# Expert biases put into PSUM by ScalarE ahead of the products, expert items of 96 rows, and the overflow branch moved behind the output store

## The chip, the cores and the metric

The kernel runs on one core of one Trainium2 chip. The metric is the time on the device, in microseconds (us), of one execution; each version is judged by the median of several runs. PE is TensorE's matmul unit, PEld its weight load, ACT is ScalarE, DVE is VectorE, POOL is GpSimd, SP is SyncE, which issues most DMAs.

## The reference, cut to what matters

One hybrid encoder layer on 512 tokens of width 1024, in float32: two kinds of attention, an output projection, and then a mixture of 32 experts of which each token uses 4. Only the last stage matters here:

```python
def expert_rows(args):
    xe, e = args
    hh = xe @ w1[e] + b1[e]
    glu = jnp.minimum(hh[:, :D_FF], SWIGLU_LIMIT)
    lin = jnp.clip(hh[:, D_FF:], -SWIGLU_LIMIT, SWIGLU_LIMIT)
    act = glu * jax.nn.sigmoid(SWIGLU_ALPHA * glu) * (lin + 1.0)
    return act @ w2[e] + b2[e]
```

`w1[e]` is 1024 x 2048 and `w2[e]` 1024 x 1024, both float32, so an expert has 12.58 MB of weights. Each expert's rows are summed into their tokens with the router's weights, and a last RMSNorm gives the output. There are 512 x 4 = 2048 (token, expert) pairs, 64 an expert on average; the router's choices, counted with the reference on its own inputs, give the fullest expert 88.

## The kernel before, in words

**Items.** The mixture is done in items, one expert with up to P = 128 of its tokens each: 32 main items (`MAIN`) and, only if some expert has more tokens than that, 15 overflow items (`REST`, `OVER`) behind a branch on `novi`. An item has 24 pieces of 128 x 1024 weights: 16 of `w1` and 8 of `w2`. For float32 accuracy each piece is split: ACT casts it to `stage_hi` (L783), DVE subtracts that from the raw piece to give `stage_lo` (L1203), and PE makes six matmuls of 512 columns (`multiply`, L2182 to L2191): hi x hi, lo x hi, hi x lo, two banks each. There are 4 stage buffers; ACT may cast piece j when PE has used piece j - 4. SP loads 1 MB chunks (two pieces) into a ring of 12 slots, each when DVE has split what was in its slot (`load_body`, L494 to L507); so a chunk is asked for about one item before its use.

**Order of an item t on each engine** (j counts pieces in `body`, pieces 0 to 15 are of `w1`, 16 to 23 of `w2`):
- PE: first bias matmuls (`bias_1`, L2150 to L2159: one 0/1 selector per bank, 32 rows deep, `start=True`), pieces 0 to 8, eight transposes of the previous item's activations (`turn_a`, L2147), pieces 9 to 15, eight transposes of the next item's gathered rows (`turn_x`, L2139), pieces 16 to 23, which belong to the previous item's second product.
- ACT: the casts, and behind piece 3 the weighted result of item t - 2 (`y_evac`, L1093), behind 12 `a_evac` (L1079), behind 19 `gate(t)` (L1085), behind 21 `x_evac` (L1063, L1066).
- DVE: the subtractions, and behind piece 1 `gated` (L1644), behind 5 `weights` (L1612), behind 7 the bias selector `select1` (L1607), behind 12 and 21 `turned_lo` (L1596), behind 18 the two clips that empty the first product's banks (L1632, L1636).
- POOL: gathers the next rows by an indirect DMA from `tn_scratch` (L655) and adds results into `x_scratch` by an indirect DMA (L666).

The biases b1 of all experts lie in SBUF as `bias1`, loaded by eight DMAs (L486) and split by ACT (L998) and DVE (L1506) before the mixture.

**Before the first item** the normalised rows `tn` are stored to `tn_scratch` tile by tile (L516), and the first gather waits for all of these stores. SP issues the loads of chunks 4 and 5 just ahead of the last of them (L511 to L516).

**The end.** The last item's result is kept in two parts and added by one-hot matmuls (`last_expert`, L2290) instead of by a scatter. Every engine reads `novi` and branches over the overflow items; then SP waits for POOL's `all_scattered` (L580), loads the four 128-row tiles of `x_scratch` (L582), DVE adds PE's sums (L1756), ACT takes the squares and roots (L1185, L1187), DVE scales (L1763) and SP stores (L585). In the last main item `gated` stands behind piece 23 (L1704) and `y_evac` behind piece 3 of the tail loop (L1159), after both halves of `a_evac`.

Of the kernel before, what the change touches and what calls it, by code (L numbers as in the profile page):

```python
# [20 lines left out]
F32 = mybir.dt.float32  # L21
# [30 lines left out]
OVER = S * TOPK // P - 1  # L52
# [78 lines left out]
def build(nc, x, norm1_g, w_in, b_f, g_fox, g_sb, w_out, norm2_g, w_router, b_router, w1, b1, w2, b2,  # L131
# [6 lines left out]
    with ExitStack() as ctx:  # L138
# [32 lines left out]
        gtab = sb("gtab", [P, ITEMS], I32)  # L171
        wtab = sb("wtab", [P, ITEMS])
        seltab = sb("seltab", [P, ITEMS + OVER])
        eidtab = sb("eidtab", [1, 16], I32)
        novi = sb("novi", [1, 1], I32)
        gidx = sb("gidx", [P, 1], I32)
        sidx = sb("sidx", [P, 1], I32)
        wcol = sb("wcol", [P, 1])
        last_rows = sb("last_rows", [P, 1])
# [47 lines left out]
        bias1 = over("bias1", [P, D], F32R, room_at)  # L227
        wdT = over("wdT", [P, S], F32R, room_at + 4096)
        sel1 = over("sel1", [P, P], F32R, room_at + 6144)
        sel1b = over("sel1b", [P, P], F32R, room_at + 6656)  # L230
        onehot = over("onehot", [P, S], F32R, room_at + 7168)
# [7 lines left out]
        ohslot = over("ohslot", [P, 16, P], F32R, qk_at + 16 * S)  # L239
        over_slot = in_slot("over_slot", [P, 16, P], F32R, 8)  # L240
# [8 lines left out]
        b1raw = slot(9)[:, 0:D]  # L249
# [5 lines left out]
        y_hi = act_hi[:, 2 * D:3 * D]  # L255
        y_lo = act_lo[:, 2 * D:3 * D]
        g2b = slot(8)[:, 0:D]
        small = slot(8)[:, D:2 * D]
        gath = qk2[:, 0, :]
        glu = qk2[:, 1, :]  # L260
        lin = qk2[:, 2, :]
        sig = qk2[:, 3, :]
        yout = qk2[:, 4, :]
# [22 lines left out]
        counts = part(2007, 32)  # L286
        most = part(2039, 1)
# [20 lines left out]
        minus, prow = cols[:, 16:17], cols[:, 17:18]  # L308
# [15 lines left out]
        g2_in, bias_in, gf_in = sem("g2_in"), sem("bias_in"), sem("gf_in")  # L324
# [26 lines left out]
        bias_hi, bias_lo = sem("bias_hi"), sem("bias_lo")  # L351
# [6 lines left out]
        sel1_r, sel1_used, clipped, sig_done, act_made = (sem(n) for n in ("sel1_ready", "bias1_added", "clipped", "sig_done", "act_made"))  # L358
# [90 lines left out]
        def _(sp):  # L449
# [78 lines left out]
            for c in range(SLOTS):  # L528
# [3 lines left out]
                if c == 1:  # L532
                    sp.wait_ge(bias_lo, 2)
# [16 lines left out]
            sp.dma_start(gfb, norm_f_g.rearrange("(a d) -> a d", a=1).partition_broadcast(P)).then_inc(gf_in, 16)  # L550
            sp.wait_ge(over_known, 1)
            n_over = sp.value_load(novi[0:1, 0:1], min_val=0, max_val=1)
            with sp.If(n_over > 0):
                sp.wait_ge(over_ready, 1)
# [4 lines left out]
                for c in range(KT):  # L559
                    z = moe_slot(c)  # L560
                    sp.wait_ge(*MAIN.freed(E - 1, c + 4))
                    sp.dma_start(slot(z), w1_d[bass.ds(e0, 1), c].rearrange("e p n -> p (e n)")).then_inc(full[z], 16)
                ew1, ew2 = expert(1), expert(0)
                for c in range(SLOTS):
                    load_body(ew1, ew2, c, REST.freed(0, c) if c < 4 else REST.freed_first(c - 4))
# [1759 lines left out]
```

## Time and profile before

| | us |
|---|---|
| median of 3 runs | 1477.76 |
| lowest, highest | 1477.41, 1479.73 |
| the profiled execution, its own time | 1478.53 |
| span of its instructions | 1476.8 |
| mean granted clock of TensorE | 0.993 of full |

The profiled execution is 0.8 us above the median; 1.7 us of its time lie outside the span. A time at the head of a timeline row is counted from the start of the span, and a row with xN merges N instructions in a row: its second number runs from the start of the first to the end of the last. A matmul's duration includes its pipeline, so the distance between starts tells its cost, not the duration.

### The profile page before, as it was taken

The page shows a single profiled execution, that of the slowest core. Times are in us where ns is not written, and L with a number is a line of the kernel's source. Part 1 is how long each engine was busy: PE and PEld are TensorE (multiplying, and loading weights), DVE is VectorE, ACT ScalarE, POOL GpSimd, SP SyncE. Part 2 cuts the span into 40 slices and gives each one's busy share as a digit, 9 for nine tenths or more (in the row PEclk, how much of TensorE's full clock was granted, in tenths as well). Part 3 has the DMA queues.
Part 4 walks back from the last instruction along what each step waited for, and adds up shares of the span by engine and source line. Part 5 has one row for each costly group of instructions (what it writes and reads, how often), then busy time and mean ns, then how long its engine had stood idle before and what let it go on. Part 6 is the DMA issues. An engine that isn't in the chain of part 4 may idle for free.

```text
span 1476.8 us, 22343 instructions
## 1 busy us (share of the span) xinstructions
PE 1448.6 (98%) x7069; PEld 1180.6 (80%) x7069; DVE 1323.5 (90%) x1520; ACT 1114.6 (75%) x1345; POOL 325.4 (22%) x179
## 2 busy tenths in 40 slices
PE   9999999999999999999999999999999999999996
PEld 7777787787888888888888888888888888888884
DVE  5778656569999999999999999999999999999997
ACT  5668545357888888888888888888888888878885
POOL 3000000141322222222222233233222222222210
PEclk9999999989999999999999999999999999999998
DMA  8021122369999999999999999999999999999963
GB/s 258 22 65 57 30 94 67 129 225 418 417 383 384 378 378 374 375 370 376 375 369 375 374 369 380 365 371 389 367 361 373 373 378 369 369 372 379 370 220 125
DMA packets 100074, 451.32 MB, mean 306 GB/s; under 512 B 13443, under 2 KB 25731, under 8 KB 67266
## 3 DMA queue, kind: packets, MB, share of 16 engines
q1 hardware_dynamic: 90706, 434.16, 76.8%
q0 software_dynamic: 9328, 16.64, 4.5%
q8 instruction: 23, 0.38, 0.1%
q14 instruction: 17, 0.14, 0.0%
HBM read 444.66 MB, written 22.54 MB: 316 GB/s over the span
## 4 chain that ended last, share of the span: by engine, by line
PE 85%; DVE 7%; ACT 3%; DMA 2%; issue 2%; POOL 0%; SPq 0%; POOLq 0%; ACTq 0%; DVEq 0%
PE zpair L2189 46%; PE bank L2189 23%; PE bank L1889 2%; PE bank L1777 2%; PE bank L2139 2%; PE bank L2147 2%; PE bank L1779 2%; PE bank L1778 2%; DVE stage_lo L1203 1%; DVE lbuf L1283 1%; PE zpair L2158 1%; DVE pt_lo L1292 1%; DMA tn_scratch<-qk 1%; ACT stage_hi L783 1%; DMA ring<-x_scratch 0%
## 5 line engine op out<-in xcount | busy, mean ns | idle before, releaser
L1203 DVE TENSOR_TENSOR stage_lo<-ring,stage_hi 128x1024 fp32r<-128x1024 f32 x796 | 945.9, 1222 | 37.9 <-ACT stage_hi L783 8.3
L783 ACT CAST stage_hi<-ring 128x1024 fp32r<-128x1024 f32 x796 | 828.2, 1054 | 169.8 <-PE zpair L2189 139.0
L2189 PE MATMUL zpair<-stage_hi,act_hi 128*128 128x512 f32 x1024 | 322.5, 396 | 0.0
L2189 PE MATMUL zpair<-stage_lo,act_hi 128*128 128x512 f32 x1024 | 316.2, 390 | 0.4 <-DVE stage_lo L1203 0.3
L2189 PE MATMUL zpair<-stage_hi,act_lo 128*128 128x512 f32 x1024 | 316.0, 390 | 0.0
L2189 PEld LDWEIGHTS zpair<-stage_lo,act_hi 128*128 128x128 f32 x1024 | 192.1, 188 | 41.8 <-DVE stage_lo L1203 1.3
L2189 PEld LDWEIGHTS zpair<-stage_hi,act_lo 128*128 128x128 f32 x1024 | 192.2, 188 | 40.9
L2189 PEld LDWEIGHTS zpair<-stage_hi,act_hi 128*128 128x128 f32 x1024 | 187.2, 188 | 43.4 <-issue 7.9
L662 POOL COPY sidx<-gtab 128x1 int32 (+1 forms) x31 | 122.4, 3947 | 378.2 <-ACT qk L1093 378.2
L2189 PE MATMUL bank<-stage_hi,act_hi 128*128 128x512 f32 x512 | 161.2, 396 | 0.0
L2189 PE MATMUL bank<-stage_hi,act_lo 128*128 128x512 f32 x512 | 158.6, 391 | 0.0
L2189 PE MATMUL bank<-stage_lo,act_hi 128*128 128x512 f32 x512 | 157.8, 389 | 0.0
L666 POOL DMA_INDIRECT x_scratch<-qk,sidx x31 | 129.6, 4179 | 25.0 <-POOL sidx L662 25.0
L2189 PEld LDWEIGHTS bank<-stage_lo,act_hi 128*128 128x128 f32 x512 | 96.1, 188 | 21.1 <-DVE stage_lo L1203 0.4
L2189 PEld LDWEIGHTS bank<-stage_hi,act_lo 128*128 128x128 f32 x512 | 96.4, 188 | 20.5
L2189 PEld LDWEIGHTS bank<-stage_hi,act_hi 128*128 128x128 f32 x512 | 94.0, 189 | 17.6
L651 POOL COPY gidx<-gtab 128x1 int32 (+1 forms) x31 | 6.1, 198 | 402.8 <-PE bank L2139 402.8
L1596 DVE TENSOR_TENSOR act_lo<-bank,act_hi 128x512 fp32r<-128x512 f32 x128 | 82.3, 683 | 4.9 <-ACT act_hi L1063 3.5
L1777 PE MATMUL bank<-act_hi,stage_hi 128*128 128x512 f32 x184 | 76.3, 415 | 1.9 <-DVE v_lo L1247 1.9
L1779 PE MATMUL bank<-act_hi,stage_lo 128*128 128x512 f32 x184 | 72.0, 391 | 0.0
L1778 PE MATMUL bank<-act_lo,stage_hi 128*128 128x512 f32 x184 | 71.9, 391 | 0.0
L675 POOL TENSOR_TENSOR qk<-ring 128x1024 f32<-128x1024 f32 x3 | 8.1, 2725 | 273.0 <-DVE ring L1352 273.0
(297 smaller groups left out, 1450.9 us busy)
## 6 DMA issues: line engine op xcount, KB each, us to landing
ring<-in_w SPq DMA_DIRECT2D x384, 1024.0 KB, 8.0
ring<-in_w_in SPq DMA_DIRECT2D x12, 1024.0 KB, 5.3
ring<-in_w_out SPq DMA_DIRECT2D x4, 1024.0 KB, 4.9
xs_all<-in_x SPq DMA_DIRECT2D x4, 512.0 KB, 6.5
ring<-in_x SPq DMA_DIRECT2D x4, 512.0 KB, 3.7
tn_scratch<-qk SPq DMA_DIRECT2D x4, 512.0 KB, 3.5
x_scratch<-ring SPq DMA_DIRECT2D x4, 512.0 KB, 3.8
ring<-x_scratch SPq DMA_DIRECT2D x4, 512.0 KB, 6.7
```

The costliest lines, as they stand in the source:

```text
L662: nc.gpsimd.tensor_copy(sidx[:], gtab[:, i:i + 1] if isinstance(i, int) else gtab[:, bass.ds(i, 1)]).then_inc(sidx_copied, 1)
L666: nc.gpsimd.indirect_dma_start(out=x2_d[:, :], out_offset=bass.IndirectOffsetOnAxis(ap=sidx[:, 0:1], axis=0), in_=yout, in_offset=None, bo ...
L783: nc.scalar.copy(dst, src).then_inc(split_hi, 1)
L1203: nc.vector.tensor_tensor(dst, src, hi_ap.bitcast(F32), ALU.subtract).then_inc(split_lo, 1)
L1596: nc.vector.tensor_tensor(dst_lo[:, 4 * h:4 * h + n, :], bank[6 + h][:, 0:n * P].rearrange("p (k t) -> p k t", k=n), dst_hi[:, 4 * h:4 * h ...
L1777: pe.matmul(dst, w_hi, m_hi, start=start, stop=False)
L1778: pe.matmul(dst, w_hi, m_lo, start=False, stop=False)
L1779: return pe.matmul(dst, w_lo, m_hi, start=False, stop=stop)
L1889: mm = pe.matmul(obank[m][:, kb * P:S], w[:, ph % 2, kb, :], x[:, m, 4 * kb:3 * kb + TT, :].rearrange("p i q -> p (i q)"), start=kb == 0 a ...
L2139: mm = pe.transpose(bank[6 + k // 4][:, k % 4 * P:(k % 4 + 1) * P], gath[:, k * P:(k + 1) * P], identF[:])
L2147: mm = pe.transpose(bank[6 + k // 4][:, k % 4 * P:(k % 4 + 1) * P], lin[:, k * P:(k + 1) * P], identF[:])
L2189: mm = pe.matmul(bank[b0 + h][:], w[:, k, :], m[:, j % STAGES, h * BANK:(h + 1) * BANK], start=start and w is T_hi and m is stage_hi, stop ...
```

## The change

- A row of b1 is no longer selected by matmuls. SP loads it for each item with two DMAs that spread 4 KB each over 96 partitions (`load_b1`), and ACT copies it into the four banks of the first product (`seed`), behind pieces 20 and 22 of the item before. PE's products then add onto it: none of them has `start=True`. At the beginning a few matmuls with `start=True` over those banks (`arm`) replace as many of `keep_busy`.
- Items have 96 rows (CAP) in place of 128. Tables, gathers, transposes, clips and copies cover 96 rows; copies of transposed rows are 384 columns wide in place of 512. The 512-column matmuls of `multiply` keep all 128 columns of their stationary tiles.
- `bias1`, `sel1`, `seltab` and what makes them are gone. `body` on PE is one loop, not two.
- The end of the kernel is done at once after the main items; reading `novi` and the branch follow the store of the output. SP waits for the last main scatter itself. `gated` of the last item moves ahead of its piece 23's end (behind piece 22), `y_evac` ahead of the second half of `a_evac`.

```diff
+CAP = 96
-OVER = S * TOPK // P - 1
+OVER = S * TOPK // CAP
@@ SP
-            sp.wait_ge(split_lo, W_IN_PIECES + 8)
-            for g in range(4):
-                for r in (32 * g, 32 * g + 16):
-                    sp.dma_start(b1raw[r:r + 16, :].rearrange("p (h n) -> p h n", h=2),
-                                 b1[0][:, g * BANK:(g + 1) * BANK].rearrange("(h e) n -> e h n", h=2)).then_inc(bias_in, 16)
+            def load_b1(e, i):
+                wait(sp, b1_set, 2 * i)
+                row = b1[0][e:e + 1, :] if isinstance(e, int) else b1[0][bass.ds(e, 1), :]
+                for h in range(2):
+                    sp.dma_start(b1b[h][0:CAP, :], row[:, h * D:(h + 1) * D].partition_broadcast(CAP)).then_inc(b1_in, 16)
...
                     sp.wait_ge(oproj, 16)
                     for c in (4, 5):
                         load_w1(0, c, moe_slot(c))
+                    load_b1(0, 0)
                 sp.wait_ge(tn_ready, t + 1)
...
                 if c == 2:
+                    load_b1(1, 1)
...
             with sp.Fori(2, E) as t:
                 for c in range(SLOTS):
                     load_body(t, t - 1, c, MAIN.freed(t - 1, c))
+                    if c == 1:
+                        load_b1(t, t)
...
+            sp.wait_ge(split_lo, MAIN.split(E - 1, W1P + W2P - 1))
+            sp.wait_ge(scattered, 16 * (E - 1))
+            totals(0)
             sp.wait_ge(over_known, 1)
             n_over = sp.value_load(novi[0:1, 0:1], min_val=0, max_val=1)
@@ ACT
-            act.wait_ge(bias_in, 128)
-            nc.scalar.copy(bias1[:], b1raw).then_inc(bias_hi, 1)
...
+            def seed(i, h):
+                act.wait_ge(b1_in, i * 32 + 32)
+                nc.scalar.copy(zpair[h][0:CAP], b1b[h][0:CAP, :].rearrange("p (b n) -> p b n", b=2)).then_inc(b1_set, 1)
...
                         if j == 19:
                             gate(t)
+                        if j == 20 and not last:
+                            seed(t + 1, 0)
                         if j == 21 and not last:
                             x_evac(t + 1)
+                        if j == 22 and not last:
+                            act.wait_ge(clipped, t * 2 + 2)
+                            seed(t + 1, 1)
...
                     if j == 2:
-                        act.wait_ge(used, ub + 24 * n - 8)
+                        y_evac(q0 + n - 2, ub + 24 * n - 8)
                         a_evac(q0 + n - 1, (1,))
-                    if j == 3:
-                        y_evac(q0 + n - 2, ub + 24 * n - 8)
@@ DVE
-            nc.vector.scalar_tensor_tensor(out=bias1[:], in0=bias1[:].bitcast(F32), scalar=minus, in1=b1raw,
-                                           op0=ALU.mult, op1=ALU.add).then_inc(bias_lo, 2)
-            nc.vector.tensor_copy(sel1[:], seltab[:, 0:1].to_broadcast([P, P])).then_inc(sel1_r, 1)
...
-                        if j == 7 and not last:
-                            select1(t + 1, both)
...
+                        if j == 22 and last:
+                            gated(t)
-                gated(q0 + n - 1)
@@ PE
+            def arm(b):
+                for h in range(2):
+                    mm = pe.matmul(bank[b][:, 2 * P * h:2 * P * (h + 1)], identB[:], masks[:], start=h == 0, stop=h == 1)
...
-                    mm = pe.transpose(bank[6 + k // 4][:, k % 4 * P:(k % 4 + 1) * P], gath[:, k * P:(k + 1) * P], identF[:])
+                    mm = pe.transpose(bank[6 + k // 4][:, k % 4 * CAP:(k % 4 + 1) * CAP], gath[:, k * P:(k + 1) * P], identF[0:CAP, 0:CAP])
...
-                    else:
-                        bias_1(t, halves)
                     pe.wait_ge(xT_lo_r, t * 2 + (1 if first else 2))
                     for j in range(W1P):
+                        if j < 2:
+                            pe.wait_ge(b1_set, t * 2 + j + 1)
```

## Rows read from the trace of the kernel before

**Rows 1.** The page, busy time of each engine

```profile
PE 1448.6 (98%) x7069; PEld 1180.6 (80%) x7069; DVE 1323.5 (90%) x1520; ACT 1114.6 (75%) x1345; POOL 325.4 (22%) x179
```

**Rows 2.** The page, the chain that ended last, by engine

```profile
PE 85%; DVE 7%; ACT 3%; DMA 2%; issue 2%; POOL 0%; SPq 0%; POOLq 0%; ACTq 0%; DVEq 0%
```

**Rows 3.** Timeline of PE over one item: start, us, engine, line, operation

```profile
881.08 0.61 PE L2189 MATMUL bank<-stage_lo,act_hi 128*128 128x512 f32 x2
881.63 0.50 PE L2158 MATMUL zpair<-bias,sel 32*128 32x512 f32 x4
...
883.57 0.63 PE L2189 MATMUL zpair<-stage_hi,act_hi 128*128 128x512 f32 x2
...
904.90 1.04 PE L2139 MATMUL bank<-identF,qk 128*128 128x128 f32 x8
...
907.16 0.62 PE L2189 MATMUL bank<-stage_hi,act_hi 128*128 128x512 f32 x2
...
916.24 0.61 PE L2189 MATMUL bank<-stage_lo,act_hi 128*128 128x512 f32 x2
916.79 0.51 PE L2158 MATMUL zpair<-bias,sel 32*128 32x512 f32 x4
```

**Rows 4.** Timeline of PE before the first item

```profile
311.67 1.04 PE L2077 MATMUL zpair<-pay,ohslot 128*128 128x32 f32 x8
```

**Rows 5.** Timeline of ACT in the same item, in brackets its idle time

```profile
907.28 1.06 ACT L1085 ACTIVATE qk<-qk 128x1024 f32<-128x1024 f32 x1 [1.12 <-DVE qk L1632]
908.24 1.98 ACT L783 CAST stage_hi<-ring 128x1024 fp32r<-128x1024 f32 x2
910.13 0.57 ACT L1063 CAST act_hi<-bank 128x512 fp32r<-128x512 f32 x1
...
911.09 4.15 ACT L783 CAST stage_hi<-ring 128x1024 fp32r<-128x1024 f32 x4
...
917.85 1.26 ACT L1093 ACTIVATE qk<-bank,wcol 128x512 f32<-128x512 f32 x2
```

**Rows 6.** Timeline of DVE in the same item

```profile
905.96 1.28 DVE L1632 TENSOR_SCALAR qk<-zpair 128x512 f32<-128x512 f32 x2
...
911.76 1.28 DVE L1596 TENSOR_TENSOR act_lo<-bank,act_hi 128x512 fp32r<-128x512 f32 x2
912.96 4.62 DVE L1203 TENSOR_TENSOR stage_lo<-ring,stage_hi 128x1024 fp32r<-128x1024 f32 x4
917.50 1.22 DVE L1644 SCALAR_TENSOR_TENSOR qk<-qk 128x1024 f32<-128x1024 f32 x1
918.63 4.62 DVE L1203 TENSOR_TENSOR stage_lo<-ring,stage_hi 128x1024 fp32r<-128x1024 f32 x4
```

**Rows 7.** Windows: busy of PE, PEld, DVE, ACT, POOL; clock; DMA share; GB/s

```profile
881.00:916.70 35.70, 35.70 (x168) 29.04 (x166) 34.70 (x37) 29.27 (x32) 9.50 (x4) 1.00 0.99 374
1425.00:1426.00 1.00, 1.00 (x6) 0.84 (x5) 1.00 (x2) 0.64 (x2) 0.00 (x0) 1.00 0.80 266
```

**Rows 8.** DMA from 330 to 345 us: rate, and us to landing

```profile
DMA packets 960, 6.23 MB, mean 416 GB/s; under 512 B 169, under 2 KB 169, under 8 KB 231
...
ring<-in_w SPq DMA_DIRECT2D x7, 1024.0 KB, 21.7
```

**Rows 9.** DMA of the whole run: KB each, us to landing

```profile
ring<-in_norm_g SPq DMA_DIRECT2D x1, 512.0 KB, 4.3
```

**Rows 10.** The chain in order of time, before the first item

```profile
310.75 8.61 DMA tn_scratch<-qk
```

**Rows 11.** Timeline of the end

```profile
1442.49 1.09 PE L2147 MATMUL bank<-identF,qk 128*128 128x128 f32 x8 [0.79 <-DVE qk L1644]
...
1446.48 1.28 ACT L1093 ACTIVATE qk<-bank,wcol 128x512 f32<-128x512 f32 x2
...
1456.90 0.10 POOL L772 MEMSET gidx<- 128x1 int32 x1 [5.39 <-issue]
...
1457.09 2.29 SPq L582 DMA_DIRECT2D ring<-x_scratch  x4
```

More of the change, by code:

```diff
@@ L285, in build @@
         w_lo = part(916, 16)
-        counts = part(2007, 32)
-        most = part(2039, 1)
+        counts = part(2013, 32)
+        most = part(2045, 1)
         pick = part(952, 256).rearrange("p (a e) -> p a e", e=E)
@@ L750, in last_scatter @@
                 pool.wait_ge(y_ready, E)
+                for t in range(TT):
+                    pool.wait_ge(fin_in[t], 16)
                 nc.gpsimd.tensor_copy(sidx[:], gtab[:, E - 1:E]).then_inc(sidx_copied, 1)
@@ L1103, in turns @@
                     return 16 * (loads_before(z) + k)
+                if b == MOE0:
+                    seed_first()
+                else:
+                    seed(q0, 0)
+                    seed(q0, 1)
                 for j in range(W1P):
@@ L1648, in run_items @@
                 ub = b - OPROJ_PIECES
-                both = run is REST
-                if run is REST:
-                    select1(q0, both)
                 for j in range(W1P):
@@ L2194, in run_items @@
                 q0, n, b, T0 = run.first, run.n, run.base, run.turn0
-                low, high = ((0,), (1,)) if run is MAIN else ((0, 1), (0, 1))
                 if b == MOE0:
-                    pe.wait_ge(bias_lo, 2)
-                    pe.wait_ge(sel1_r, 1)
-                    bias_quarters((4, 5, 2, 3), range(4))
+                    for z in (4, 5, 2):
+                        arm(z)
+                    arm(3).then_inc(armed, 1)
                     pe.wait_ge(tables, 1)
@@ L2202, in run_items @@
                     weight_table((0, 1))
-                    keep_busy(0, 3)
+                    keep_busy(0, 1)
+                    arm(0)
                     pe.wait_ge(counts_read, 1)
-                else:
-                    bias_1(q0, low)
                 turn_x(q0)
@@ L2209, in run_items @@
                     weight_table((2,))
-                    keep_busy(0, 6)
+                    for _ in range(3):
+                        arm(0)
                 pe.wait_ge(xT_lo_r, 2 * q0 + 1)
                 for j in range(W1P):
+                    if j < 2:
+                        pe.wait_ge(b1_set, 2 * q0 + j + 1)
                     if j == W2P:
@@ L2217, in run_items, with body @@
                         turn_x(q0 + 1)
+                        pe.wait_ge(wt_added, 1)
+                        arm(1).then_inc(armed, 1)
                 if b != MOE0:
                     turn_x(q0 + 1)
-                def body(r, halves, first=False, last=False):
+                def body(r, first=False, last=False):
                     t = r + q0
-                    if first and b == MOE0:
-                        pe.wait_ge(sel1_r, 2)
-                        pe.wait_ge(wt_added, 1)
-                        bias_quarters((0, 1), (0, 1))
-                    else:
-                        bias_1(t, halves)
                     pe.wait_ge(xT_lo_r, t * 2 + (1 if first else 2))
                     for j in range(W1P):
-                        if j == 1 and first and b == MOE0:
-                            pe.wait_ge(clipped, 1)
-                            bias_quarters((2, 3), (2, 3))
+                        if j < 2:
+                            pe.wait_ge(b1_set, t * 2 + j + 1)
                         if j == W2P and first:
@@ L2249, in body @@
                             turn_a(t)
-                body(1, low, first=True)
-                if run is MAIN:
-                    with pe.Fori(2, 16) as r:
-                        body(r, low)
-                with pe.Fori(16 if run is MAIN else 2, n - 1) as r:
-                    body(r, high)
-                body(n - 1, high, last=True)
+                body(1, first=True)
+                with pe.Fori(2, n - 1) as r:
+                    body(r)
+                body(n - 1, last=True)
                 pe.wait_ge(aT_lo_r, 2 * (q0 + n) - 1)
@@ L2276, in _ @@
                 second_biases(t)
+            pe.wait_ge(onehot_r, TT)
+            pe.wait_ge(last_hi, 2)
+            for t in range(2):
+                last_expert(t, y_hi)
+            pe.wait_ge(y_ready, E)
+            for t in range(2):
+                last_expert(t, y_lo)
+            for t in range(2, TT):
+                if t == TT - 1:
+                    second_biases(t)
+                last_expert(t, y_hi)
+                last_expert(t, y_lo)
             pe.wait_ge(over_known, 1)
```

297 lines of the change are left out of this document (142 added, 155 removed).

## The prediction, made before the change was run

> **What bounds the kernel now.** I read the page first. PE is busy for 98% of the span [rows 1] and holds 85% of the chain that ended last [rows 2], so an operation off PE's queue is a gain unless something else is late. But DVE is at 90% [rows 1], and in the item from 881 to 917 us it is busy for 34.70 of 35.70 us [rows 7], so little needs to change for DVE to lead. The DMA share there is 0.99 at 374 GB/s: three resources are close together.
>
> Then PE's own timeline of that item [rows 3]. From one bias row to the next, 881.63 to 916.79, is 35.16 us. Piece 17 starts at 907.16 and the last third of piece 23 at 916.24: 9.08 us for 6 2/3 pieces, 1.362 us a piece. The transposes start at 904.90 and piece 17, one piece later, at 907.16: 2.26 - 1.362 = 0.90 us for eight. From the last third of one item (881.08) to the second piece of the next (883.57) are 2.49 us; without the bias it would be a third (0.454) and a piece (1.362): the bias costs 0.67 us. Check: 24 x 1.362 + 2 x 0.90 + 0.67 = 35.16.
>
> **Part 1, the bias leaves PE.** Bound by PE alone, an item takes 34.49 us, 0.67 less.
>
> **Part 2, the same work on ACT.** Two copies of 1024 columns come to stand behind pieces 20 and 22, where ACT is already behind: before 907.28 it waited 1.12 us for the clips [rows 5]. No row has ACT writing PSUM. The nearest, a cast of the same width, takes 0.945 us from start to start (908.24 to 910.13 for two [rows 5]); the dearest ACT row of that width, two scaled halves from PSUM, 1.16 us (its 1.26 less the pipeline's 0.1). I take 0.945, with nothing and 1.16 each as ends. The Trainium skill, "ScalarE: Activation LUTs", section "Step-by-step: what each stage is for", says that ScalarE reaches PSUM faster than SBUF; no row here shows that, and by it the sum would lean to the shorter end.
>
> Now the chain of that stretch, with PE's clock of rows 3 left as it is up to the transposes. ACT: gate at 907.28, cast 20 at 908.24, seed at 909.18, cast 21 at 910.13, the two copies of rows at 911.07 (0.48 each before, 911.09 - 910.13 for two; 384 of 512 columns: 0.36), cast 22 at 911.79, seed at 912.74, cast 23 at 913.68, its data at 914.78. Before, that cast was done by some 913. DVE subtracts at a step of 1.13 us (4.62 for four, less 1.22, over three [rows 6]): piece 23 from 914.78, the next item's pieces 0 and 1 from 915.91 and 917.04, `gated` from 918.17 (1.13 [rows 6]), piece 2 from 919.30 to 920.52. PE without the bias starts the next item at 904.90 + 0.90 + 8 x 1.362 = 916.70 and wants that piece's low part two pieces and two thirds later, at 920.33. It waits some 0.23 us. Pieces 23, 0 and 1 come in time by 0.1 to 0.5 us; behind piece 2 DVE gains 0.23 us a piece and catches ACT again before the clips. So the new wait stands at piece 2, on `stage_lo`, and the item takes 34.72 us: 0.44 us saved. Each tenth more in a seed adds 0.2 to the wait, each tenth less takes 0.2 away until none is left.
>
> **Part 3, 96 rows.** DVE loses the selector (0.2 us) and a quarter of four subtractions (911.76 to 912.96 is 1.20 for two of them [rows 6], so 0.15 each); both are in the chain above only where they stand, outside of it they are slack. PE's transposes stream 96 columns in place of 128. Eight transposes merge to 1.04 us [rows 3], and so do eight matmuls with only 32 moving columns [rows 4]; the moving width does not set the cost, the stationary load does, and that stays 128 wide. I take 0; the ends are 0 and a quarter of 0.90 for eight. The gather, scatter and weight DMAs carry the same real rows.
>
> **Part 4, DMA.** 374 GB/s over 35.16 us are 13.15 MB an item; the b1 rows add 2 x 96 x 4096 B = 0.79 MB. The ceiling shows where the queue is long: 416 GB/s from 330 to 345 us [rows 8], so 31.6 us for what there is now. What a spread row costs shows in the last broadcast of the kernel: 266 GB/s at a share of 0.80 [rows 7], 333 GB/s at a full share, so 2.4 us for 0.79 MB. 34.0 us an item is under 34.7: the DMA stays hidden, barely. Two costs remain. The loads of the start land after 21.7 us [rows 8]; that queue was worked off at 3.6 us an item (35.16 - 31.6) and is now at 0.7. A chunk is asked for an item ahead, so it is never late, but the b1 row of item t is asked for behind piece 3 of item t - 1 and wanted by ACT behind its piece 20, some 21 us later. For the first few items it may be late once; a wait there lets the queue shrink. I take 1 us in all, ends 0 and 5.
>
> **Part 5, before the first item.** `load_b1(0, 0)` is queued ahead of the last `tn` store. That store is on the path to the end: issued at 310.75, it lands 8.61 us later [rows 10], behind two chunks, and the first gather waits for it. 0.79 MB more in front cost 1.9 us at 416 GB/s, 2.4 at 333; less 0.3 for narrower copies: +1.8. The cover for `arm` (8 short matmuls, in place of 4 bias ones and of `keep_busy`) and for the first seeds is this same wait, many us long; `bias1`, its loads and its split leave places where PE was the path, and give nothing. The first `body` loses two half biases and waits for a clip and a seed instead: -0.3.
>
> **Part 6, the end.** `gated` moves ahead of a subtraction, so the 0.79 us for which PE waited before the last transposes [rows 11] goes. `y_evac` (1446.48 [rows 11]) loses one cast and one half copy in front of it, 0.94 + 0.48 = 1.4 us; the scatter behind it lands that much earlier, and SP, which saw POOL's branch and memset (1456.90) before its loads at 1457.09 [rows 11], waits for the scatter alone: 1.1 us more. What is late next is DVE's chain of four additions and scalings, which starts with the first tile. Reading `novi` and branching now stand behind the last scaling and store, up to 1 us where the store itself does not cover them; I take 0.3. Sum: -0.8 - 1.4 - 1.1 + 0.3 = -3.0.
>
> **Sum**, against the profiled execution's 1478.5 us: 30 items x -0.44 = -13.2; -0.3, +1.0, +1.8, -3.0. That gives 1464.8 us; the median of the runs stands 0.8 below that execution, so I forecast 1464.
>
> **Rivals.** (a) PE stays the bound: seeds cost well under 0.9 us, or the chain has slack that I don't see. 30 x 0.67 = -20.1, no other change: 1457; if the transposes also shrink by 0.22 for eight, twice an item, 1444 at the very best. For it: most rows are spaced as drawn, and 0.23 us is little. Against: pieces 23 to 1 had only 0.1 to 0.5 us left.
> (b) The chain through ACT eats it all: seeds of 1.16 us each add 0.43, an item takes 35.15, and 1464 + 30 x 0.43 = 1477, within 0.2% of no change; a little more and it is 1480. The same figure results if a spread row moves at 214 GB/s: 31.6 + 3.7 = 35.3 us an item.
> (c) Slower: the DMA queue becomes the bound through the spread rows. Alone, 512 KB of such a broadcast took 4.3 us [rows 9], 6.6 us for 0.79 MB; if that is a rate and not latency, an item takes 31.6 + 6.6 = 38.2 us, 3.0 more than now, and the kernel about 1477 + 30 x 3.0 = 1567. It decides from 3.6 us for the two loads on. Against it: the 333 GB/s of rows 7. The Trainium skill, "DMA: Bandwidth & Descriptors", section "Where 436 GB/s comes from", holds that about 358 GB/s from HBM bind a core, by which any added byte would lengthen the item; the trace disagrees, with 416 GB/s in rows 8.
> (d) The change does not do what it says: an expert with more than 96 tokens would bring 21 overflow items, 21 x 34.7 = 730 us more. The fullest has 88, so this is near nothing.
>
> **How the numbers follow.** About 0.2% (3 us) is what a measurement of this kernel can tell from no change. Forecast 0.48, from 1459 to 1471; (a) 0.22; (b) 0.17, of it 0.08 still faster, 0.06 the same and 0.03 slower; (c) 0.12; (d) 0.01. Faster 0.78, same 0.06, slower 0.16. The range takes in the forecast, nearly all of (a) and most of (b): 1450 to 1479; what is left out is (c), (d) and the far ends.
>
> **What would show it.** The distance of an item on PE, 34.7 us (34.5 in (a), over 35.1 in (b) and (c)). No rows of 32 x 512; the copies to zpair at 0.9 to 1.1 us; a wait of PE at piece 2 for `stage_lo` of some 0.2 us an item. DMA near 400 GB/s, landings of w chunks that fall slowly from over 20 us. The last `tn` store landing 10.5 us after its issue; at the end SP's loads about 2.5 us after where PE's last piece would put them now. The forecast is wrong if PE waits at piece 0 or 1 for a seed, if ACT waits for b1's DMA in most items, or if PE never waits at all.

## The result, and the profile after

The changed kernel takes 1625.8 us (median of 4 runs, 1615.9 to 1632.6) against 1477.6 beside it: a ratio of 1.0996, 95% interval 1.0922 to 1.107. It is 10% slower, where 1464 was forecast, within 1450 to 1479. The profiled run took 1632.5 us, with a span of 1630.7; it is one of the longer two of the four.

The page of the changed kernel, engines, rate and the chain that ended last, answers to [rows 1, 2]:

```profile
PE 1484.9 (91%) x6951; PEld 1201.6 (74%) x6951; DVE 1301.2 (80%) x1483; ACT 1151.7 (71%) x1409; POOL 410.3 (25%) x178
GB/s 233 27 52 78 53 78 25 262 333 374 352 347 355 340 348 341 343 345 348 336 345 346 343 329 354 353 356 341 351 355 358 344 363 347 355 338 358 362 294 114
DMA 47%; PE 14%; DVE 11%; ACT 10%; SPq 9%; issue 8%; ACTq 1%; POOL 0%; DVEq 0%; POOLq 0%
DMA b_lin<-in_b 45%; SPq L500 6%; DVE stage_lo L1252 5%; ACT stage_hi L800 5%; PE bank L1917 2%; PE bank L1805 2%; PE zpair L2204 2%; ACT zpair L1098 2%; SPq L485 2%; PE bank L1807 2%; PE bank L1806 2%; PE bank L2204 1%; ACT act_hi L1077 1%
```

PE had 85% of the chain and has 14%; 45% now belong to one kind of transfer, the second of the two b1 loads. Yet the GB/s line has fallen, to some 345 from the 374 of [rows 7]: more bytes were asked for and fewer came per us. Both facts need a reason.

The same in windows (columns as in [rows 7]), first the middle of the kernel, then two stretches of one item:

```profile
400.00:1500.00 1100.00, 1001.17 (x4389) 812.47 (x4389) 918.51 (x931) 822.69 (x905) 335.52 (x110) 0.94 0.99 348
902.00:910.00 8.00, 8.00 (x42) 6.71 (x41) 7.65 (x9) 6.42 (x8) 3.81 (x1) 1.00 1.02 202
914.00:920.00 6.00, 5.79 (x26) 4.47 (x24) 3.94 (x5) 2.00 (x2) 2.70 (x2) 1.00 1.02 416
```

The last two numbers of a line are the share of the DMA engines and their GB/s. The share is full in all three, the rate is not: 202 GB/s in one stretch and 416 four us later. So the share tells nothing of how fast the packets go.

The chain in order of time, start and length of each piece:

```profile
890.99 3.22 SPq L500
...
894.45 0.14 issue
894.58 1.03 SPq L500
...
895.89 0.33 SPq L485
...
896.41 26.48 DMA b_lin<-in_b
```

And timelines of ACT and of PE behind it, with idle time in brackets:

```profile
915.47 1.03 ACT L800 CAST stage_hi<-ring 128x1024 fp32r<-128x1024 f32 x1
922.91 1.01 ACT L1098 COPY zpair<-b_glu 96x1024 f32<-96x1024 f32 x1 [6.40 <-DMA b_lin<-in_b]
...
926.49 1.02 ACT L1098 COPY zpair<-b_lin 96x1024 f32<-96x1024 f32 x1
927.44 4.85 ACT L800 CAST stage_hi<-ring 128x1024 fp32r<-128x1024 f32 x5
```

```profile
924.95 1.22 PE L2204 MATMUL bank<-stage_hi,act_hi 128*128 128x512 f32 x2 [5.16 <-ACT stage_hi L800]
```

A closed loop: SP issues the b1 load behind the chunks of the item, it lands 26.5 us later, ACT stands before its first seed for 6.4 us with cast 21 queued behind it, PE runs dry for 5.2 us, DVE's subtractions, which free the ring slots, come late with the casts, and so SP issues the next chunks and the next b1 load late. From 400 to 1500 us ACT's wait comes 27 times (who waited for whom: us in total, times, the longest):

```profile
DVE stage_lo L1252 <- ACT stage_hi L800: 159.1, 72, 7.4
ACT zpair L1098 <- DMA b_lin<-in_b: 132.0, 27, 6.8
```

PE's pause also costs clock. Behind the pause that ends at 924.95 the granted clock is at half (the 1.2 GHz level) from 924.4 to 927.8, and the starts of two-matmul steps stand 0.85 to 1.02 us apart in place of 0.45. The mean of the long window above is 0.94 of full speed; in the item of [rows 7] it was 1.00. In all, the clock stood at half for 172 us of the changed kernel and for 22 us of the kernel before.

### The profile page after: what moved, and what is told of

Same layout as the page of the kernel before. It is cut to its first block, busy times and chain, and to the rows that moved or that the text cites. A ratio compares the mean times of both kernels' runs of the same rounds, so it can differ in the third digit from the quotient of the medians.

```text
span 1630.7 us, 22339 instructions
## 1 busy us (share of the span) xinstructions
PE 1484.9 (91%) x6951; PEld 1201.6 (74%) x6951; DVE 1301.2 (80%) x1483; ACT 1151.7 (71%) x1409; POOL 410.3 (25%) x178
## 4 chain that ended last, share of the span: by engine, by line
DMA 47%; PE 14%; DVE 11%; ACT 10%; SPq 9%; issue 8%; ACTq 1%; POOL 0%; DVEq 0%; POOLq 0%
DMA b_lin<-in_b 45%; SPq L500 6%; DVE stage_lo L1252 5%; ACT stage_hi L800 5%; PE bank L1917 2%; PE bank L1805 2%; PE zpair L2204 2%; ACT zpair L1098 2%; SPq L485 2%; PE bank L1807 2%; PE bank L1806 2%; PE bank L2204 1%; ACT act_hi L1077 1%; DVE lbuf L1332 1%; SPq L505 1%
## 5 line engine op out<-in xcount | busy, mean ns | idle before, releaser
L677 POOL COPY sidx<-gtab 96x1 int32 (+1 forms) x31 | 170.9, 5512 | 485.4 <-ACT qk L1121 485.4
L2204 PE MATMUL bank<-stage_hi,act_hi 128*128 128x512 f32 x512 | 189.2, 455 | 108.4 <-ACT stage_hi L800 108.4
L2204 PEld LDWEIGHTS bank<-stage_hi,act_hi 128*128 128x128 f32 x512 | 108.0, 223 | 141.6 <-ACT stage_hi L800 121.1
L2204 PE MATMUL bank<-stage_lo,act_hi 128*128 128x512 f32 x512 | 179.1, 435 | 0.7 <-DVE stage_lo L1252 0.4
L2204 PE MATMUL bank<-stage_hi,act_lo 128*128 128x512 f32 x512 | 177.8, 432 | 0.0
L1098 ACT COPY zpair<-b_glu 96x1024 f32<-96x1024 f32 x31 | 31.4, 1012 | 146.3 <-DMA b_lin<-in_b 145.1
L2204 PEld LDWEIGHTS bank<-stage_lo,act_hi 128*128 128x128 f32 x512 | 109.0, 215 | 29.3 <-DVE stage_lo L1252 4.6
L2204 PEld LDWEIGHTS bank<-stage_hi,act_lo 128*128 128x128 f32 x512 | 109.5, 214 | 26.5
L666 POOL COPY gidx<-gtab 96x1 int32 (+1 forms) x31 | 17.2, 554 | 361.2 <-PE bank L2167 261.6
```

The costliest lines, as they stand in the source:

```text
L677: nc.gpsimd.tensor_copy(sidx[:], gtab[:, i:i + 1] if isinstance(i, int) else gtab[:, bass.ds(i, 1)]).then_inc(sidx_copied, 1)
L1098: nc.scalar.copy(zpair[h][0:CAP], b1b[h][0:CAP, :].rearrange("p (b n) -> p b n", b=2)).then_inc(b1_set, 1)
L2204: mm = pe.matmul(bank[b0 + h][:], w[:, k, :], m[:, j % STAGES, h * BANK:(h + 1) * BANK], start=start and w is T_hi and m is stage_hi, stop ...
```

## The experiments

Beside these kernels the kernel before took 1477.5 to 1479.7 us (medians). Where an interval stands, a kernel has four runs (experiment 1 has two); the others are single runs, and a difference of a few us between two of them says nothing.

**1. No b1 loads after the first item.** The seeds stay; from item 1 on they copy item 0's biases, so most biases are not those of their expert.

```diff
 def load_b1(e, i):
+    if not (isinstance(i, int) and i == 0):
+        return
 ...
-    act.wait_ge(b1_in, i * 32 + 32)
+    act.wait_ge(b1_in, 32)
```

> The changed kernel with the two b1 loads of item 0 alone; every later item adds item 0's bias row again, so the biases of the other experts are left out. All else, the copies into PSUM too, stays. Theory 1 (the spread loads cost the DMA: reads of one HBM row by all 16 engines slow everything that is in flight): the item falls from about 40 us to 34.5 to 34.8 us and the time to my sum without the DMA terms, 1463 us (1455 to 1470). Theory 2 (the loads cost only because they queue behind the weights and land too late): the same time here. Theory 3 (the copies on ACT and the wait for them cost it): it stays over 1550 us.

Measured: 1469.4 us, ratio 0.9944 (0.9922 to 0.9967). One item on PE:

```profile
901.72 0.83 PE L2168 MATMUL bank<-identF,qk 96*128 96x96 f32 x8
917.45 0.72 PE L2205 MATMUL zpair<-stage_lo,act_hi 128*128 128x512 f32 x2
936.48 0.83 PE L2168 MATMUL bank<-identF,qk 96*128 96x96 f32 x8
```

936.48 - 901.72 = 34.76 us an item, and 34.72 was forecast. All 156 us of the loss are the loads, or waits that they bring; with the rest of the change an item is shorter than the 35.16 us before.

**2 and 3. Is it the one hot row?** All 96 packets of a load read the same 4 KB of memory. Two kernels read other addresses (a weight's rows, which then stand in place of the biases), 96 distinct rows in the one and 16 rows six times each in the other. The edit of experiment 2:

```diff
-    row = ... b1[0][bass.ds(e, 1), :]
+    row = ... w1_d[bass.ds(e, 1), 0].rearrange("e p n -> p (e n)")
 ...
-        sp.dma_start(b1b[h][0:CAP, :], row[:, h * D:(h + 1) * D].partition_broadcast(CAP))
+        sp.dma_start(b1b[h][0:CAP, :], row[0:CAP, h * D:(h + 1) * D])
```

> The same two loads per item, of the same size and at the same place in the queue, but each of the 96 partitions gets another HBM row (taken from w1, so the biases are replaced by other numbers). Theory 1 (one row read by all engines): no stretch in which 8 KB packets take 700 ns in place of 311, 400 GB/s and more at a full share, 1465 us (1455 to 1475). Theory 2 (place in the queue and lead): nothing changes, 1590 to 1630 us. Theory 3b (96 destination rows or 4 KB packets are what is slow): nothing changes either, and the 700 ns packets stay.

> The same loads, but from 16 HBM rows (of w1, in place of the biases) that are read six times each, so that an engine reads one row of its own. Theory 1 in its narrow form (what is slow is that many engines read the same bytes at once): as with 96 rows, 1465 us. Theory 1 in its wide form (each repeated read of a row is slow): between, 1500 to 1600 us.

Measured: 1614.6 and 1623.2 us, one run each, beside 1615.9 to 1632.6 for the changed kernel. The source of the rows makes no difference that these runs can tell. That theory falls.

**4. Biases back on PE**, with the 96-row items and the new end kept: `bias_1`, `select1` and their tables as before, `seed` and `load_b1` gone.

> The changed kernel with the bias matmuls of the kernel before put back (selectors, bias1, its loads and split, the bias slots on PE), so that only the 96-row items and the moved end remain. By my sum: the end -3.0, the narrower copies before the first item -0.3, transposes 0: 1474.5 us. If the transposes shrink with their moving columns (0.61 us for eight in the changed kernel's trace in place of 0.79 from first start to the next product), 0.18 x 2 x 31 = 11 us more: 1463 us. If the end gained nothing: 1477.

Measured: 1467.0 us, ratio 0.9923 (0.9905 to 0.9942), all outputs computed. A part of the change that was thought to give nothing in the items, the 96-row transposes, is the gain there, and the part that the change is named for gives none: even with its DMAs taken away (1469.4, interval of the ratio 0.9922 to 0.9967) it is not ahead of this one.

**5. The place in the queue.** The loads of items 2 and up leave SP's queue; ACT issues them behind piece 1 for the item after.

```diff
-    if c == 1:
-        load_b1(t, t)
+    if j == (3 if first else 1) and not last and b == MOE0:
+        act.wait_ge(b1_set, 2 * t + 2)
+        for h in range(2):
+            act.dma_start(b1b[h][0:CAP, :], ...partition_broadcast(CAP)).then_inc(b1_in, 16)
```

> The same two loads for every item, with the same bytes and the same 96 rows, but issued by ScalarE from item 2 on (behind piece 1 for the item after) and so not in SyncE's queue of weights. Theory A (place in the queue: the 24 us from issue to landing is the backlog of weights ahead of the loads, and the seed waits for that): the seeds are ready in time, about 1465 to 1475. Theory B (96-row transfers put the 16 DMA engines out of step and their throughput falls to about 345 GB/s whoever issues them): still about 1600 to 1630, now with SyncE's weights late. Theory C (the bytes alone, 0.79 MB an item over what the engines could spare): between 1580 and 1630, with the weights' landing time up instead of the biases'.

Measured: 1557.6 us: 68 of the 156 us of loss are gone, 88 are not. None of the three theories had that number. ACT no longer waits for the seeds' data, but for weights: 166 us from 400 to 1400 us, in 147 waits. This kernel is also the one in which the biases' packets can be seen by themselves, since they have a queue of their own. Windows, columns as above; the biases flow in the second and the fourth:

```profile
902.00:910.00 8.00, 7.58 (x39) 6.30 (x39) 8.00 (x10) 5.36 (x6) 1.39 (x2) 1.00 1.03 427
920.00:926.00 6.00, 6.00 (x27) 4.65 (x27) 6.00 (x7) 3.85 (x6) 4.05 (x1) 1.00 1.02 292
940.00:946.00 6.00, 5.58 (x29) 4.51 (x29) 6.00 (x6) 4.82 (x5) 0.28 (x2) 1.00 1.01 418
958.00:964.00 6.00, 6.00 (x27) 4.69 (x26) 6.00 (x6) 5.63 (x7) 3.94 (x1) 1.00 1.02 292
```

The packet records of the trace, counted by queue and size in two us each (number, mean ns of one; by its size a packet of 8 KB is a piece of `w1`, one of 4 KB in the weights' columns a piece of `w2`):

```
from us   weights 8 KB   weights 4 KB   biases 4 KB
904         48  309       112  160          -
922         28  449        31  237        51  230
924         27  453        45  227        48  224
940         43  316       115  159          -
```

While 96-row packets flow, every packet takes some 1.45 times as long, the weights' too. The biases don't only take their own time; they hold up whatever flows beside them. In the changed kernel's slow stretch (902 to 910 us) a weight packet of 8 KB took 595 to 702 ns, as means over two us each. Why it is held up more there than beside a second queue, no run shows.

**6. All 128 partitions.** The loads go where the weights go, to 128 rows, with a third more bytes (32 rows of it used by nobody).

```diff
-    sp.dma_start(b1b[h][0:CAP, :], row[:, h * D:(h + 1) * D].partition_broadcast(CAP))
+    sp.dma_start(b1b[h][:], row[:, h * D:(h + 1) * D].partition_broadcast(P))
```

> The loads go to all 128 partitions as the weights' do (each DMA engine 8 rows instead of 6): a third more bytes, 1.05 MB an item. Theory B (out of step through the shape): about 1465 to 1490. Theory C (bytes): slower than the changed kernel, 1640 to 1680. Theory A (place in the queue): unchanged within 1 percent, 1610 to 1640.

Measured: 1513.7 us. 33% more bias bytes, 112 us less time, though 24 us more than theory B allowed.

**7. 96 rows, an eighth of the bytes.** 128 columns of each half from item 1 on; the others stay item 0's.

> The loads of items 1 and up bring 128 of the 1024 columns of each half (512 bytes a row instead of 4 KB), so most biases stay those of item 0; the number of loads, their place and their 96 rows stay. Theory C (bytes): about 1466 to 1475. Theory B (shape): still over 1550, for each load leaves the engines as unequal as before. Theory A (place in the queue): the issue is as far behind the backlog as before, so the seeds stay late by about as much, 1560 to 1630; if the backlog goes with the bytes, A falls with C's number.

Measured: 1469.8 us, as without loads. So a 96-row transfer is harmless when it is short, and the backlog ahead of the load (a chunk landed after a median of 17.3 us) doesn't hurt by itself. Theory A of these expectations, the place in the queue, falls as a cause of its own; and so does B as it was put, in which the shape of each load costs whatever its length.

**8. The same bytes and counts as in 6, each load cut into rows 0 to 63 and 64 to 127.**

```diff
+    for p in (0, P // 2):
+        sp.dma_start(b1b[h][p:p + P // 2, :], row[:, h * D:(h + 1) * D].partition_broadcast(P // 2))
 ...
```

> The loads to all 128 partitions (1513.7 us as one transfer each), but each cut into two transfers of 64 rows: the same 1.05 MB an item and the same 4 KB packets, and over the two transfers every DMA engine again has 8 rows. Theory D (a transfer of other than 128 rows deals its rows to the engines in another way than the weights do, so that two engines write to the same partitions, and all packets that flow beside them are held up): slow, 1620 to 1720. Theory B as first put (engines that get 6 rows beside 8 fall out of step, whatever the partitions): about 1514, since the counts are equal. Theory C (bytes alone): 1514.

Measured: 1702.3 us, 189 more than with whole loads of the same bytes, packets and source; only the number of transfers differs too, four an item for two. One of its stretches:

```profile
936.00:942.00 6.00, 6.00 (x33) 5.02 (x32) 5.54 (x5) 4.95 (x6) 2.81 (x2) 1.00 1.04 221
```

The share is full and the packets themselves are slow: in the two us from 938 the weights' 8 KB packets took 634 ns and those of 4 KB, biases and weights together, 317. A mere cost of issuing more transfers would leave them as they are. So what costs is how a transfer's rows lie over the partitions. The Trainium skill, "SBUF — State Buffer", section "Door 1: The DMA port swizzle (why `[64,N]` ≈ `[32,N]`)", states that partitions 0 to 63 reach only 8 of SBUF's 16 DMA ports and 64 to 127 the other 8. By that map a transfer of 64 rows would crowd onto half of the ports, and one of 96 would send two thirds of its rows there; the weights, which need the same ports, would queue behind them. That is an inference. The runs agree in order (64 rows worse than 96, 96 worse than 128) and in that the weights' packets are held up; which engine writes which partition, and so what happens at the ports, no record here shows.

The gathers of the changed items are such transfers too: they have 96 indices for 128 before. From 400 to 1400 us a gather's packet took 159 ns (median, the scatters' packets of some 327 ns left out) in the kernel before and in experiment 11, which is experiment 4 with 128 indices, and 228 ns in experiment 4. In the microseconds of a gather the weights' 8 KB packets took 309 ns in experiment 11 and 368 in experiment 4. So the change slowed the queue in a second place, which cost nothing as long as the queue had room (experiments 4 and 11: 1467.0 and 1467.1 us).

**9. The changed kernel's bytes in the shape of 6:** 128 rows of 768 columns from item 1 on, 0.79 MB an item (a quarter of the biases stay item 0's).

> One transfer of 128 rows each again, but 768 of the 1024 columns (3 KB rows) from item 1 on: 0.79 MB an item, exactly the bytes of the changed kernel (a quarter of the biases stay those of item 0). If the bytes by themselves cost what the sustained 392 GB/s of the 128-row kernel says, (12.58 + 0.53 + 0.79) MB / 392 GB/s = 35.5 us an item, 0.7 over the 34.75 without the loads: about 1485 to 1495, over the kernel before. If bytes had room up to the 416 GB/s that the prediction took: 1469. If the bytes of the changed kernel were the loss and not its rows: over 1580.

Measured: 1495.3 us. So 1495.3 - 1469.4 = 26 us of the loss are bytes and 1625.8 - 1495.3 = 130 us are the 96 rows with the loop of waits and the lost clock that they bring. (One run, and the changed kernel's own runs lie up to 17 us apart.) From 400 to 1400 us, this kernel's window and then that of experiment 6:

```profile
400.00:1400.00 1000.00, 989.01 (x4494) 782.93 (x4493) 935.80 (x956) 839.18 (x927) 495.69 (x113) 1.00 1.01 391
```

```profile
400.00:1400.00 1000.00, 980.73 (x4421) 767.73 (x4420) 919.45 (x939) 821.19 (x907) 489.96 (x111) 1.00 1.01 392
```

Both are at a full share, with PE waiting, at the same rate: 391 to 392 GB/s is what the DMA engines sustain with this kernel's mix of weights, scatters and 96-row gathers. That it would be the same with gathers of 128 indices is not shown.

**10. The 128 rows in ACT's queue.**

> The 128-row loads issued by ScalarE as in the kernel at 1557.6 us. Theory D with C: no packets are held up any more while the biases flow (over 390 GB/s in these stretches instead of about 290), and the time is set by bytes, about 1505 to 1520, place in the queue being worth under 10 us. Theory A (place in the queue counts beside the rows): clearly under the 1513.7 of the same loads in SyncE's queue, 1470 to 1495.

Measured: 1511.7 us, 2 less than in SP's queue, which single runs can't tell from nothing. The first and last of these windows are those in which the biases flow:

```profile
933.00:939.00 6.00, 6.00 (x27) 4.65 (x26) 6.00 (x6) 5.84 (x8) 3.44 (x1) 1.00 1.02 413
940.00:944.00 4.00, 4.00 (x19) 3.30 (x19) 3.67 (x4) 2.30 (x3) 3.19 (x2) 1.00 1.03 422
968.00:974.00 6.00, 6.00 (x25) 4.42 (x25) 6.00 (x6) 5.42 (x8) 2.37 (x1) 1.00 1.02 414
```

413 GB/s where the same queue with 96 rows had 292, and the packet records give 313 ns for 8 KB beside the biases. The place in the queue matters only while the rows are wrong.

**11. The end.** The forecast had -3.0 us for it; in every kernel with the new end, but for experiment 13, it is longer. From the start of PE's last transposes to the end of the span: 1476.8 - 1442.49 = 34.3 us before, 1630.7 - 1595.12 = 35.6 after, 1465.9 - 1430.10 = 35.8 in experiment 4 (whose last transposes start at 1430.10). The chain of experiment 4 there:

```profile
1433.71 1.18 POOL sidx L673
...
1435.65 10.79 DMA x_scratch<-qk,sidx
...
1446.50 0.34 SPq L556
```

In the kernel before the same scatter lands in 6.03 us:

```profile
1449.74 6.03 DMA x_scratch<-qk,sidx
```

It is issued 1.7 us sooner behind the transposes (1435.65 - 1430.10 = 5.55, before 1449.74 - 1442.49 = 7.25), and lands 4.8 us later behind its issue. First suspect: 96 indices in place of 128. The index tables get 128 rows again, the last 32 out of bounds. In short:

```diff
-gtab, gidx, sidx = [CAP, ...]
+gtab, gidx, sidx = [P, ...]
+memset(gtab[CAP:P, :], int(AWAY))
-in_=yout
+in_=qk2[:, 4, :]
```

> The kernel at 1467.0 us (biases on PE, 96-row items), but gathers and scatters are given 128 indices again, rows 96 to 127 out of bounds and so skipped, as in the kernel before. Theory: the software DMA of 96 indices costs GpSimd longer before its first packet (in the last scatter 7.3 us from issue to first packet against 2.3 before, landing 10.8 against 6.0 us), which sits on the path at the end, and the first gather's 1.9 against 1.2 us at the start. Then the last scatter lands in about 6 us and the time falls by 4.7 + 0.7 us to about 1461.5. Rival: the longer landing comes from something else at the end (what the earlier scatter waits for, the fin loads), and the time stays within 1 us of 1467.

Measured: 1467.05 us, ratio 0.9927 (0.991 to 0.9943): nothing, the scatter's issue takes 6.84 us and it lands in 11.38. The theory of the indices falls.

**12. GpSimd against VectorE.** In experiment 4 GpSimd's issue, and VectorE beside it:

```profile
1435.65 6.70 POOL L677 DMA_INDIRECT x_scratch<-qk,sidx  x1 [0.78 <-POOL sidx L673]
```

```profile
1437.55 3.48 DVE L1220 TENSOR_TENSOR stage_lo<-ring,stage_hi 128x1024 fp32r<-128x1024 f32 x3
1440.95 0.15 DVE L1741 CAST last_rows<-gtab 96x1 f32<-96x1 int32 x1
1441.13 1.22 DVE L1743 TENSOR_TENSOR act_hi<-b2raw,act_hi 32x1024 fp32r<-32x1024 f32 x1
```

1435.65 + 6.70 = 1442.35 = 1441.13 + 1.22: GpSimd gets done when VectorE's unbroken run does. The same coincidence stands in the changed kernel (1600.70 + 6.70 against 1606.17 + 1.22). To test it, VectorE waits behind the copy of the last weights until GpSimd is done.

```diff
@@ scatter
+if isinstance(i, int) and i == E - 2:
+    pool.sem_inc(gath_zero, 1)
@@ VectorE, last item
     weights(q0 + n - 1)
+    dve.wait_ge(gath_zero, 2)
```

> The kernel at 1467.0 us (biases on PE, 96-row items) with one wait more: behind the copy of the last weights, VectorE waits until GpSimd has finished issuing the scatter of the item before the last. Theory: GpSimd's issue of that scatter took 6.70 us from 1435.65, to the moment when VectorE's unbroken run of subtractions (SBUF to SBUF) ended at 1442.35, because the two engines are not served together; with VectorE idle it takes about 1.1 to 1.8 us (1.77 in the kernel before, where it fell into a shorter run), the scatter lands some 6 us after its issue and not 10.8, and SyncE's loads of the end start about 4 us earlier. VectorE and PE finish about 1 us later, and VectorE's additions wait for PE's last products too, so the time falls by only 1 to 3 us, to about 1465. Rival: the issue takes 6.7 us whatever VectorE does (a cost of the moved end itself, as the 128 indices, which changed nothing, would also allow); then VectorE loses 5 us of the tail and the time rises to 1470.

Measured: 1467.4 us, ratio 0.9928 (0.9911 to 0.9944), issue 6.70 us again. It says nothing: GpSimd's sequencer raised the semaphore at 1434.86, before its engine began at 1435.08, and VectorE never waited.

**13. The same, with the semaphore raised by a memset that GpSimd executes behind the issue.**

```diff
-    pool.sem_inc(gath_zero, 1)
+    nc.gpsimd.memset(gidx[:], 0).then_inc(gath_zero, 1)
```

> The kernel with the wait again, which had passed at once (GpSimd's sequencer raised the semaphore at 1434.86, before its engine began the issue at 1435.08; the issue again lasted 6.70 us, to 1441.78, the end of VectorE's unbroken run). The semaphore is now raised by a memset that GpSimd executes behind the issue. Theory (the issue is held up by VectorE's run): the issue takes 1.8 to 3.5 us, the scatter lands by about 1442, SyncE's loads start about 3 us earlier, and the time stays within 2 us of 1467, because VectorE's last subtractions come 1 to 2 us later. Rival (6.7 us whatever VectorE does): VectorE idles until 1441.8, its subtractions and with them the end come 4 to 5 us later, about 1471.

Measured: **1461.85 us**, ratio 0.989 (0.9873 to 0.9906), all outputs computed: the best of all, 5 us under experiment 4 and better than the expected 1465 to 1469. Timelines of GpSimd and VectorE, then the chain:

```profile
1434.89 3.23 POOL L677 DMA_INDIRECT x_scratch<-qk,sidx  x1 [0.78 <-POOL sidx L673]
1437.63 0.61 POOL L681 MEMSET gidx<- 96x1 int32 x1
```

```profile
1438.27 3.50 DVE L1222 TENSOR_TENSOR stage_lo<-ring,stage_hi 128x1024 fp32r<-128x1024 f32 x3 [1.40 <-POOL gidx L681]
```

```profile
1434.89 7.26 DMA x_scratch<-qk,sidx
```

A wait of 1.40 us on VectorE shortens the issue from 6.70 to 3.23 us and the landing from 10.8 to 7.3. From the last transposes (1429.35) to the end of the span are now 1461.1 - 1429.35 = 31.8 us for 35.8: 4 of the 5 us lie there. The rival (6.7 us whatever VectorE does) falls. The Trainium skill, "SBUF — State Buffer", section "Who interferes with whom", says that VectorE and GpSimd share a pair of SBUF ports, and that a VectorE instruction with both inputs in SBUF holds up GpSimd's reads; the subtractions are of that kind, and the timelines agree. The same section of the Trainium skill infers that such an instruction doesn't hold up the writing of a DMA's descriptors; here the issue of the scatter was held up all the same, and the measurement decides. What stays open is the kernel before: its issue took 1.77 us from 1449.74 although VectorE subtracted from 1450.05 to 1453.54. When an issue gets through beside such a run, no run here shows.

## Why the prediction was wrong

**The failed step is Part 4**, "34.0 us an item is under 34.7: the DMA stays hidden, barely", in both of its terms.

*The ceiling.* 416 GB/s was read from one stretch of 15 us [rows 8]. In the kernel before it held on to 400 us, gathers included (one flows in the first of these windows, one in the second), but up to there no scatter's packets had flowed:

```profile
350.00:355.00 5.00, 5.00 (x22) 3.32 (x21) 3.69 (x5) 3.91 (x5) 0.19 (x1) 1.00 1.01 415
385.00:390.00 5.00, 5.00 (x24) 3.48 (x22) 5.00 (x7) 4.67 (x6) 0.00 (x0) 1.00 1.02 408
390.00:395.00 5.00, 5.00 (x26) 4.06 (x23) 5.00 (x5) 4.43 (x6) 2.88 (x1) 1.00 1.04 415
```

Over whole items of the changed kind the engines gave 391 to 392 GB/s at a full share (experiments 6, 9, 10). Two things differ: the loop has scatters, and the change itself slows the gathers (behind experiment 8), for which Part 3 had "the same real rows" and no price. How the difference divides between them is open. 13.15 MB then need 33.5 us and 0.79 MB more make 35.6; experiment 9 gave 35.68 and 35.34 us for two successive items. The right ceiling alone would have turned the forecast into 1477.6 + 30 x (35.56 - 35.16) - 0.3 + 1.8 - 3.0, about 1488, slower than before; experiment 9 measured 1495.3.

*The price of the rows.* 2.4 us for 0.79 MB came from 333 GB/s in the last broadcast [rows 7]. The reading was off: in that microsecond 53 packets of 4 KB took 162 ns each, as the weights' do, beside 12 of a scatter at 327 ns, which pull the rate down. It was a load to 128 rows with few others in flight, and what it could not show is what 96 rows do to others. From the first transposes to the last, the changed kernel takes 1595.12 - 328.51 = 1266.6 us, experiment 1 takes 1432.57 - 328.37 = 1104.2: over 30 items 5.4 us more each, 40.2 in place of 34.76. Of these 5.4, the bytes are 0.9 (26 us in experiment 9), the 96 rows 4.5. The 1 us in all for b1 rows that come late rested on the same two figures: ACT waited for them in 27 items from 400 to 1500 us, 132 us in sum, and the wait did not let the queue shrink but brought itself about anew in each item.

**Rival (c)** had the right bound, the DMA queue through the spread rows, and its price of 38.2 us an item and 1567 us was nearer than the forecast, but still short, and its reason (6.6 us for the rows themselves; from its own row, 4.3 us for 512 KB, it is 6.45) was not the mechanism. It got 0.12. The doubt about it rested on the same row as the forecast. The condition written under "what would show it" came true: ACT waits for b1's DMA in most items. The 358 GB/s from HBM that the rival takes from the Trainium skill, "DMA: Bandwidth & Descriptors", section "Where 436 GB/s comes from", do not bind here: 392 GB/s flowed over a millisecond.

**Parts 1 to 3, with the loads taken away (experiment 1).** 34.76 us an item for 34.72, but by luck: two misses cancel. *Part 3:* the transposes did shrink. From 901.72 to the second piece behind them at 903.78 are 2.06 us, less a piece (1.362) 0.70 for eight in place of 0.90, so 0.40 an item where 0 was taken; the end of the range, a quarter of 0.90, was nearly right. *Part 2:* a seed takes 1.01 us, 0.95 from start to start, as forecast (0.945) from the cast into SBUF; but PE's wait for `stage_lo` comes to 34.76 - (34.49 - 0.40) = 0.67 us and not 0.23 (the forecast's own times, 920.52 against 920.33, give 0.19), spread over several pieces such as the one at 917.45. What Part 1 took off PE (0.67) was all given back there. Experiment 4 shows the same from the other side: bias on PE, transposes short, 35.16 - 0.40 = 34.76, and 923.52 to 958.30 on PE is 34.78.

**Part 5.** Forecast +1.8 before the first item; PE's first transposes start at 328.51 in the changed kernel and 324.97 before, +3.5. The store in the chain:

```profile
310.95 11.30 DMA tn_scratch<-qk
```

It has 2.7 us more than [rows 10] (forecast 1.9 to 2.4). The other 0.9 are GpSimd's next step, `pay_weights`, 2.69 for 1.77 us.

**Part 6.** Forecast -3.0 of which -0.8 lies before the last transposes; measured +1.3 behind them. The copies in front of `y_evac` went as said (the scatter is issued 1.7 us sooner for 1.4), but its issue took 6.70 us in place of 1.77, held up by VectorE's subtractions (experiment 13); without that hold-up the end is 34.3 - 31.8 = 2.5 us shorter than before, where -2.2 of the forecast lay there. Which other terms of Part 6 hold was not tested one by one. Sum for experiment 1 from its own rows: first transposes 328.37 - 324.97 = +3.4; first to last (1432.57 - 328.37) - (1442.49 - 324.97) = -13.3; end +1.3; together -8.6, the difference of the spans (1468.2 - 1476.8).

## What to carry to other kernels

Bytes are not all a DMA costs. In this kernel, whose queue is full, a transfer to 96 or 64 partitions held up the transfers beside it, while one to all 128, rows nobody reads included, did not: spread over 128 or keep it short. The same goes for a gather. Read the ceiling of the DMA from a long stretch at full share that contains every kind of transfer of the loop, never from a burst; a full share says nothing of the rate. And when a DMA that GpSimd issues is on the path, look at what VectorE does in those microseconds: a wait of 1.4 us there was worth 4 to 5 us.

## What had not been expected of the hardware

- Packets of 8 KB that normally take 309 ns took 449 beside 96-row packets, and a mean of up to 702 ns in the changed kernel; the same biases as two transfers of 64 rows cost 189 us more than as one of 128 (1702.3 against 1513.7).
- Where the 96 rows came from in memory (one row, 16, or 96 of them) made no difference (1625.8, 1623.2, 1614.6).
- Eight transposes of 96 rows in place of 128 cost 0.70 us in place of 0.90.
- A gather with 96 indices in place of 128 had packets of 228 ns in place of 159 (experiments 4 and 11), and the 8 KB packets beside it took 368 ns in place of 309.
- GpSimd's issue of the last indirect DMA took 6.70 us under VectorE's subtractions (6.84 with 128 indices) and 3.23 with a pause of VectorE in it.
